# Choice and gate table in one stage with 80 candidate pairs per head, 67 early up products instead of 97, and late ones spread through the experts

## The reference, cut to what matters

```python
q = (xt @ w_q).reshape(t, PEER_HEADS, 2, PEER_HALF)               # 8 heads, 2 halves of 128
sc = jnp.einsum("thpc,hpnc->thpn", q, sub_keys)                   # 128 sub-keys per half
top_s, top_i = lax.top_k(sc, PEER_TOPK)                           # 16 of 128, 16 lists
cand_s = top_s[:, :, 0, :, None] + top_s[:, :, 1, None, :]        # 16 x 16 pairs per head
best_s, best_pos = lax.top_k(cand_s.reshape(t, 8, 256), PEER_TOPK)
idx = ...            # expert = first key * 128 + second key
gate = jax.nn.softmax(best_s, axis=-1)
act = jnp.einsum("cd,ced->ce", xc, u[ic])                         # 128 chosen experts per token
hid = jax.nn.gelu(act, approximate=False) * gc
out = jnp.einsum("ce,ced->cd", hid, v[ic])
```

## Time and profile before

| | us |
|---|---|
| median of 3 runs | 2569.49 |
| lowest, highest | 2559.23, 2578.27 |
| the profiled execution | 2563.19 |
| its span | 2561.4 |
| TensorE busy | 2373.8 (93%) |
| VectorE busy | 1385.9 (54%) |
| ScalarE busy | 733.4 (29%) |
| GpSimd busy | 397.8 (16%) |

### The profile page before, as it was taken

How to read it: one execution, slowest core, us unless ns; L and a number is a source line. 1 busy time by engine, 2 the same in 40 slices (tenths; PEclk the granted TensorE clock), 3 DMA queues, 4 the chain that set the end, 5 groups by cost and what they waited for, 6 DMA issues and landing times. The chain is left out here.

```text
span 2561.4 us, 26540 instructions
## 1 busy us (share of the span) xinstructions
PE 2373.8 (93%) x10097; PEld 1729.5 (68%) x10097; DVE 1385.9 (54%) x2491; ACT 733.4 (29%) x1327; POOL 397.8 (16%) x305
## 2 busy tenths in 40 slices
PE   7989899899999988888989999999995999989889
PEld 4457666686555555656568888889994898875444
DVE  1335423427987966556267777766676624434331
ACT  1134312322111043525233333333333322211110
POOL 1100000000323233232021111123331000013100
PEclk9999999999999999999989999999997999989899
DMA  4231132113877768786899999977772322120110
GB/s 182 94 95 38 54 132 99 70 62 107 272 254 242 247 194 259 228 261 209 269 366 309 316 311 310 310 257 283 274 280 74 132 99 97 68 107 33 50 66 33
DMA packets 183343, 457.32 MB, mean 179 GB/s; under 512 B 15664, under 2 KB 106032, under 8 KB 176432
## 3 DMA queue, kind: packets, MB, share of 16 engines
q1 hardware_dynamic: 146352, 321.38, 37.2%
q0 software_dynamic: 36864, 134.23, 15.3%
HBM read 408.17 MB, written 47.38 MB: 178 GB/s over the span
## 5 line engine op out<-in xcount | busy, mean ns | idle before, releaser
L759 PE MATMUL bank<-XT,ur 128*128 128x384 f32 x1552 | 524.5, 495 | 28.8 <-DMA ur<-in_u 28.5
L759 PEld LDWEIGHTS bank<-XT,ur 128*128 128x128 f32 x1552 | 293.5, 193 | 233.4 <-DMA ur<-in_u 44.7
L1261 PE MATMUL bank<-Vh,Hh 128*128 128x512 f32 x768 | 299.9, 390 | 13.6 <-DVE Hl L1312 13.6
L1262 PE MATMUL bank<-Vl,Hh 128*128 128x512 f32 x768 | 300.0, 391 | 0.0
L1263 PE MATMUL bank<-Vh,Hl 128*128 128x512 f32 x768 | 299.9, 390 | 0.0
L794 POOL DMA_INDIRECT ring_c<-in_v,gidx x128 | 148.0, 1156 | 501.4 <-DVE x_res L806 389.4
L1310 DVE TENSOR_TENSOR Vl<-Vr,Vh 128x1024 fp32r<-128x1024 f32 x128 | 156.8, 1225 | 116.7 <-ACT Vh L1284 112.1
L1284 ACT ACTIVATE Vh<-Vr 128x1024 fp32r<-128x1024 f32 x128 | 135.5, 1059 | 249.9 <-PE bank L1263 221.2
L1261 PEld LDWEIGHTS bank<-Vh,Hh 128*128 128x128 f32 x768 | 144.6, 188 | 44.3 <-DVE Hl L1312 14.9
L768 ACT ACTIVATE ar<-bank 128x384 f32<-128x384 f32 x97 | 47.5, 490 | 428.8 <-PE bank L759 419.5
L1090 DVE TENSOR_TENSOR hot<-tab_sb,ijg 128x1024 f32<-128x1024 f32 x96 | 113.0, 1218 | 105.1 <-PE bank L1116 98.5
(11 more groups left out here) (306 smaller groups left out, 4076.5 us busy)
## 6 DMA issues: line engine op xcount, KB each, us to landing
ur<-in_u SPq DMA_DIRECT2D x128, 512.0 KB
Vr<-in_v SPq DMA_DIRECT2D x128, 512.0 KB, 5.2
W<-in_w_stream SPq DMA_DIRECT2D x27, 2048.0 KB, 7.5
gates<-stage SPq DMA_DIRECT2D x48, 512.0 KB, 6.3
Gr<-gates SPq DMA_DIRECT2D x128, 192.0 KB
early<-ar SPq DMA_DIRECT2D x97, 192.0 KB
A<-early SPq DMA_DIRECT2D x97, 192.0 KB
w_raw<-in_w_mixer SPq DMA_DIRECT2D x14, 1024.0 KB, 4.9
```

Source lines behind the costliest of these rows:

```text
L759: mm = pe.matmul(c.bank[bank + r][:, 0:DN], c.ur[:, r, k * P:(k + 1) * P], c.XT[:, k, 0:DN], start=k == 0, stop=k == KT - 1)
L1261: pe.matmul(ps, Hh[r][:, tok], Vh[r][:, cut], start=n == 0, stop=False)
L1262: pe.matmul(ps, Hh[r][:, tok], Vl[r][:, cut], start=False, stop=False)
```

## The change

1. The scores move into `phase_query`: after query group g+1, TensorE scores group g for all four tiles (8 records); both ScalarE and VectorE copy scores. The keys have a buffer and a DMA of their own.
2. `phase_choose` and `phase_gates` become `phase_table`. The order is: choose tile 3 (gathered), choose 0, choose 1, slices 0, choose 2, slices 1, slices 2. Its buffers lie in the weight ring `c.W`, in `XT` and in `SC`.
3. 80 candidate pairs per head (2x16, 2x8, 4x4, 8x2) instead of 256; the pair is got back from the position with shifts (11 small operations instead of 3).
4. In `choose`, 9 dots lie in the first links and 14 behind the last one-hot sum; slices have none; 12 dots before slices 2; 14 more at the head of the experts, the remaining 33 among them.
5. ScalarE weighs 5 tokens of a slice, VectorE 3.
6. Early products: (9, 13, 13, 13), 4 in each tile's slices, 4 between slices 1 and slices 2, 3 at the end, 67 in all. Stores: 2 per product after slices 0, 4 per product after slices 1, all 16 at once after slices 2.
7. In the experts 61 are late: the first three, then every second or third, never two in a row from the fifth on. ScalarE makes `Uh` of the next but one right behind the gelu. The dots and adds are spread by a weight of 8 per late and 3 per early expert.

```diff
-E_CHOOSE = (10, 16, 16, 16)
-E_LOOP, E_GAP = 4, 9
-E_GATES = sum(E_CHOOSE)
-EARLY = E_GATES + DT * (E_LOOP + E_GAP)
-DOTS_CHOOSE = 63
-DOTS_GAP = 6
+PAIRS = 5 * TOPK
+E_SCORE, E_SLICES, E_DRAIN, E_LAST = (9, 13, 13, 13), 4, 4, 3
+EARLY = sum(E_SCORE) + DT * E_SLICES + E_DRAIN + E_LAST
+LATE = PK - EARLY
+DOTS_LINK, DOTS_TAIL, DOTS_DRAIN, DOTS_FIRST = 9, 14, 12, 14
+DOTS_TABLE = DT * (DOTS_LINK + DOTS_TAIL) + DOTS_DRAIN
...
+                f = g - 1
+                pe.wait_ge(qd if f % 2 else qa, f // 2 + 1)
+                if f >= 4:
+                    pe.wait_ge(sd if f % 2 else sa, f // 2 - 1)
+                for tt in range(TT):
+                    cut = slice(tt * P, (tt + 1) * P)
+                    mm = pe.matmul(c.bank[4 + f % 4][:, tt * PK:(tt + 1) * PK], qT[:, f % 2, cut], keys[:, f], start=True, stop=True)
+                mm.then_inc(sg, 1)
...
+def phase_table(c, ijg, early, SC, gat):
...
+        # sync
+            turns(E0, EH0 + E_SLICES)
+            sp.wait_ge(copied, 2 * NSL)
+            for i in range(E_SCORE[3]):
+                for j in range(2 * i, min(2 * i + 2, CUTS)):
+                    store(0, j)
+                early.turn(sp, E3 + i)
+            turns(EH1, E_SLICES)
+            sp.wait_ge(copied, 4 * NSL)
+            for i in range(E_DRAIN):
+                for j in range(i * CUTS // E_DRAIN, (i + 1) * CUTS // E_DRAIN):
+                    store(1, j)
+                early.turn(sp, ED + i)
+            turns(EH2, E_SLICES)
+            sp.wait_ge(copied, 6 * NSL)
+            for j in range(CUTS):
+                store(2, j)
+            turns(EL, E_LAST)
...
+        # tensor
+            products(E0, E_SCORE[0])
+            products(E1, E_SCORE[1])
+            turn(1)
+            products(E2, E_SCORE[2])
+            turn(2)
+            slices(0, EH0)
+            products(E3, E_SCORE[3])
+            turn(3)
+            slices(1, EH1)
+            products(ED, E_DRAIN)
+            slices(2, EH2)
+            products(EL, E_LAST)
...
+                for a0, na, nb in ((0, 2, 16), (2, 2, 8), (4, 4, 4), (8, 8, 2)):
+                    o = cand[:, :, put:put + na * nb].rearrange("p h (a b) -> p h a b", b=nb)
+                    left = first[:, :, a0:a0 + na].unsqueeze(3).broadcast_to([P, PH, na, nb])
+                    right = second[:, :, 0:nb].unsqueeze(2).broadcast_to([P, PH, na, nb])
+                    last = dve.tensor_tensor(o, left, right, ALU.add)
+                    put += na * nb
...
+                dots(count["room"] + DOTS_TAIL - count["dot"])
+                gates(n)
...
+            choose(0)
+            for n in (1, 2):
+                count["room"] = count["dot"] + DOTS_LINK
+                choose(n)
+            slices(0)
+            count["room"] = count["dot"] + DOTS_LINK
+            choose(3)
+            slices(1)
+            dots(DOTS_DRAIN)
+            slices(2)
...
 def phase_experts(c, early, gat):
...
+    HEAD = 3
+    late = [p < HEAD or (p - HEAD) * (LATE - HEAD) % (PK - HEAD) < LATE - HEAD for p in range(PK)]
...
+        work = [8 * lates[p + 1] + 3 * (p + 1 - lates[p + 1]) for p in range(PK)]
+        due = [OPS * w // work[-1] for w in work]
...
+            # tensor, expert p
+                if p == 0:
+                    up(1)
+                    up(2)
+                elif p + 1 >= HEAD and p + 1 < PK and late[p + 1]:
+                    up(lates[p + 1])
...
+            # scalar, expert p
                     act.activation(A[r][:], c.bank[m % 2][:, 0:DN], ACT.Gelu).then_inc(gelud, 1)
+                    hi_u(m + 2)
...
+            # vector, ahead of expert 0
+            s, done = DOTS_TABLE, 0
+            for i in range(DOTS_FIRST):
+                if i == DOTS_FIRST // 2:
+                    lo_u(2)
+                gat.dot(dve, s)
+                s += 1
```

More of the change, by code:

```diff
@@ L913, in _, with turns, store @@
         @block.sync
         def _(sp):
+            def turns(e, n):
+                for i in range(n):
+                    early.turn(sp, e + i)
+            def store(tt, j):
+                cut = slice(j * PK // CUTS, (j + 1) * PK // CUTS)
+                sp.dma_start(dest[:, cut, tt * P:(tt + 1) * P], stage[:, cut]).then_inc(early.tabled, 16)
             early.load(sp, 0)
             early.load(sp, 1)
-            for e in range(E_GATES):
-                early.turn(sp, e)
+            turns(E0, EH0 + E_SLICES)
@@ L1131, in weigh, with slices @@
                 last.then_inc(weighed_a, 1)
[L1133 to L1134 removed]
+            def slices(tt, e):
                 weigh(tt * NSL)
                 if tt >= 1:
[L1137 removed]
+                    act.wait_ge(early.tabled, 16 * CUTS * tt)
                 for s in range(NSL):
@@ L1169, in _, with scored @@
-        @block.gpsimd
-        def _(pool):
-            for s in range(DOTS_CHOOSE, SLOTS):
-                gat.fetch(pool, s)
-def phase_experts(c, gat):
+                    if s % (NSL // E_SLICES) == NSL // E_SLICES - 1:
+                        early.gelu(act, e + s * E_SLICES // NSL, EB)
+            def scored(n, e):
+                k = E_SCORE[n] - 4
+                gelus(e, k)
+                exped(n)
+                gelus(e + k, 4)
+                if n >= 1:
+                    turned(n)
@@ L1181, in phase_experts @@
+def phase_experts(c, early, gat):
     nc, t = c.nc, c.t
-    LATE = PK - EARLY
     RV = 3
+    HEAD = 3
+    late = [p < HEAD or (p - HEAD) * (LATE - HEAD) % (PK - HEAD) < LATE - HEAD for p in range(PK)]
+    lates = [sum(late[:p]) for p in range(PK + 1)]
+    assert lates[PK] == LATE
+    index = [EARLY + lates[p] if late[p] else p - lates[p] for p in range(PK)]
+    reads = [sum(not late[q] for q in range(p % RV, p + 1, RV)) for p in range(PK)]
     with ExitStack() as ctx:
@@ L1189, in phase_experts @@
         Ul = [sb(f"Ul{i}", [P, KT, P], F32R) for i in range(2)]
+        A = [sb(f"A{i}", [P, DN]) for i in range(RV)]
+        ring = sb("ring", [P, RG, D])
         Vr = [sb(f"Vr{i}", [P, D]) for i in range(RV)]
@@ L1316, in _ @@
-                lo_u(m + 2)
-                due = SLOTS if n == PK - 1 else min(SLOTS, 2 * min(n + 1, EARLY) // 3 + 2 * max(0, n + 1 - EARLY))
-                while done < due:
+                if late[p] and p > 0:
+                    lo_u(lates[p] + 2)
+                while s < SLOTS and s - DOTS_TABLE - DOTS_FIRST < due[p]:
+                    gat.dot(dve, s)
+                    s += 1
+                if p == turn + 2:
+                    dve.wait_ge(gat.gelud, 1)
+                    dve.wait_ge(cleared, 1)
+                    dve.tensor_tensor(gat.hid[:], gat.hid[:], gat.gate[:], ALU.mult).then_inc(gat.gated, 1)
+                    dve.wait_ge(gat.gated, 1)
@@ L1319, in _ @@
+                while p > turn + 2 and done < SLOTS and DOTS + done < due[p]:
                     gat.add(dve, done, acc[:] if done % 2 else c.X[:, GT])
```

595 lines of the change are left out of this document (293 added, 302 removed).

## The result

The changed kernel takes 2598.07 us (2591.44 to 2605.86, six runs), the kernel before beside it 2567.06 (2559.23 to 2578.27): a ratio of 1.0109, with a 95% interval of 1.0087 to 1.0131. I had forecast 2560 us, 3 less than the profiled execution of the kernel before; by the ratio it is 28 us slower. The profiled execution took 2598.08 us, its span 2595.9.

What follows compares the result with a forecast made beforehand. TensorE and VectorE were taken as nearly level, TensorE bounding the experts. First main at 1137.4 + 769.7 of products + 38 of waits = 1945 against 1947.6, so 2563.2 - 3 = 2560 us; range 2515 to 2600.

Steps and rivals of the forecast that it cites:

- gap 0: Between slices 0 and slices 1: 13 products, eight at 6.4 us beside stores, 77 us, level with VectorE's 77.1.
- gap 1 and slices 2: Behind slices 1: 14.3 MB at some 370 GB/s, 38.5 us until stage is free, TensorE waiting some 10; slices end at 1070.2.
- end of the table: After slices 2: last u issued behind all 16 stores, 28 us with the load; TensorE waits some 17, ends at 1103.4.
- start of the experts: Before the first main: u lands, splits, 14 dots on VectorE; 34 us, of which TensorE works 12.6; first main at 1137.4.
- TensorE's ledger: From 585 to the last main: 1234 us of work and 126 standing, against 1261 and 102 before; products alone give -29.4 us.
- the places of the waits: TensorE stands: query's end and choice 25 us, gap 0 11, gap 1 12, table's end 17, experts' start 21, experts 38.
- the cause that I gave: In late experts with an early neighbour, Hl comes 4.31 us after the up against one main of 4.13; 17 us in all.
- ten at 1.7: In the experts, about ten places where two early ones follow a late one: TensorE waits 1.7 us each, 17 in all.
- rival 3: DMA rate decides: gap 0 costs 10 us more, gap 1 50 instead of 38.5, the end 5 more; 2586 us, chance 0.16.
- The tails: 14 dots in a row behind a choice tile's last sum, eight waiting for GpSimd's fetches: 20.5 us, bounds 16.0 and 25.2.
- Rivals 1 and 2: 1: waits hidden in experts, 2510 us, chance 0.27. 2: VectorE late for late experts' gelu, 2630 or 2600 us, 0.15.
- rival 2: In the experts, VectorE's adds make it late for late experts' gelu: +70 us, 2630, or 2600 if half do; chance 0.15.

Runs made afterwards that it cites:

- the late block: Changed kernel with its 58 remaining late experts in one row at the end instead of every second or third: ratio 0.9965 to the kernel before.
- the move of Uh: Changed kernel with ScalarE splitting a late expert's next u behind Hh instead of ahead of Vh, expert 0 excepted: ratio 1.0014 to the kernel before.
- The two kernels on gap 0: Changed kernel without dots and gathers in the choice's third tile: gap 71.2 us; changed kernel with an eighth of the stores behind slices 0: gap 80.8 us.
- short tails: Changed kernel with two dots instead of 14 behind each tile of the choice, the other 36 done in the experts: ratio 1.0072 to the kernel before.
- three edits and short tails: Changed kernel with late experts in one row, last u ahead of 12 stores, two dots before expert 0 and two behind each tile: 2522.37 us, ratio 0.9811.

## Why the prediction was wrong, step by step

| step | predicted | measured | miss |
|---|---|---|---|
| choice begins | 601.5 | 602.4 | +0.9 |
| first tile | 45.4 | 45.6 | +0.2 |
| second, third tile with tails | 78.0, 77.1 | 85.9, 79.0 | +9.8 |
| slices 0 and 1 | 51.2 each | 50.6, 48.2 | -3.6 |
| gap 0 | 78.0 | 88.9 | +10.9 |
| gap 1 and slices 2 | 83.8 | 92.7 | +8.9 |
| end of the table | 33.2 | 40.9 | +7.7 |
| start of the experts | 34.0 | 36.9 | +2.9 |
| experts, to the end of the last main | 807.7 | 804.9 | -2.8 |

These add up to 34.9 us (the slices' begin, four us behind the third tile, was right). Another 2.2 lie behind the last main, where both kernels do the same. Together they are the 37.1 us between the span that the forecast meant (2561.4 less 2.6) and the 2595.9 measured.

**What was right.** TensorE's ledger, the choice's tile, the slices (3.08 us each, 3.2 forecast), the places of the waits but for one of 8.06 us for a `u` in gap 1, and the experts' total, which the late block and the move of Uh trace to the cause that I gave. Its parts were mixed: 20 us on isolated late experts instead of 17, and 13 at nine places that I had counted as ten at 1.7. That the total came out within 3 us is partly luck.

**The step that failed** is the sum's treatment of the DMA engines: "I take 6.4 us for each of the eight: 51 + 26 = 77 us, level with VectorE's", and "some 370 GB/s are 38.5 us, and `stage` is not free before". I put 9 of the third tile's 23 gathers beside the eight products with stores, and left the five products behind them at 5.2 us. In these 26 us lie the 14 gathers of the tail and five loads and gelus, 10.9 MB by my own sizes: 420 GB/s, for which the sum has no term, where 338 were reached over the gap. Measured are 54.8 and 30.5 us, and 3.7, of which I had only 0.8: the rest of the slices' product and the step to the next slices. The stage came free 46.0 us behind slices 1 (1004.6 to the end of TensorE's wait at 1050.56), in which 15.2 MB went at 330 GB/s, not 14.3 at 370. TensorE waited 20.9 us for the last `u`, not 17. These three places are 27.5 of the 34.9 us. The two kernels on gap 0 show the size of it: stores without gathers 71.2 us, both 88.9.

This is rival 3, the DMA rate, to which I gave 0.16: it had 10, 11.5 and 5 us more in these three places; measured are 11, 7.5 and some 4 in the wait with 3 in the product behind it. I weighed it too low because the earlier trace rows showed a full DMA share with TensorE never idle. The share was full in gap 0 too (0.97 over 867 to 957): it tells nothing of how late one given transfer is. What made a given `u` late has no term of its own in the sum: in gap 0 its way from issue to landing, 12.1 us ahead of the longest wait and 6.0 to 7.8 in the tail instead of 4.0; in gap 1 the 13.65 us in which SyncE was held at the issue of the stores ahead of it. Only at the end did I count the stores ahead, 28 us with the load, and it took 32.5 from the last slice to the product's start.

**The tails.** I took 20.5 us for 14 dots, between bounds of 16.0 and 25.2. Measured are 25.7, 23.3 and 23.2. Two dots in the second tile's links waited 3.9 us for rows besides; the sum has nothing for them. The first tail reaches the upper bound, which is also what the rule of the Trainium skill ("SBUF — State Buffer", "SBUF: two separate sides") would give. But its rows show something else than a fetch of 1.99 us each time: most of the late fetches took 0.94 us, and VectorE waited for rows that had been issued but had not landed (in this tail the median from issue to landing was 9.3 us for rows in `W` and 9.8 for rows in `SC`). The runs don't separate the two.

**The clock.** I named a fall of the clock in the new gaps as something that would make me wrong, and put nothing into the sum for it. In the earlier trace rows the granted clock is 0.98 to 0.99; in the changed kernel's stages 0.96, 0.96, 0.71 and 0.79. After the wait of 20.85 us TensorE ran at half speed, 1.2 instead of 2.4 GHz, for 6.1 us, after the 6.24 for 5.4, and so on, eleven times between 603 and 1180 us, 50 us of matmuls in all. In the same stages of the kernel before there were seven, 26 us in all. At half of these lengths, the changed kernel loses 25 us by it and the one before 13: 12 us of the difference, which lie in the misses above beside the waits. They are worked out from these rows; no run isolates them.

**Rivals 1 and 2.** The waits were not hidden; they could have been (the late block). VectorE was not late for the gelu of late experts: it waited for all 58 of them, 195.3 us in all, and moving Uh alone would else have changed nothing.

The range, 2515 to 2600, held the time by 2 us, which is luck: its upper end came from rival 2, which is not what happened. The sign I had wrong. Of the chances, "slower by over 1%" had 0.18.

## What to carry to other kernels

Sum all bytes that fall into a stretch, gathers included, and hold them against the rate that was reached with full engines (330 to 340 GB/s here). Then price a transfer that someone waits for by its place in its queue and by how long the issue of what stands ahead of it takes. Where a run of stores, gathers and a load that TensorE needs meet, ask first whether the gathers can go elsewhere. When an order is spread evenly, look at the shortest distance between an operation and its user that it creates, not at the mean: 35 us of waiting, 20 of them as 0.35 us on each of 56 neighbours, ate the whole gain of 29 us in TensorE's ledger, and one instruction moved on an engine that is busy 264 of 805 us gave most of it back. Behind each wait of several microseconds, add the slow product that follows it.

## What was unexpected of the hardware

Issuing is not free when the DMA engines are full. A store of the last row of 16 took 24.40 / 16 = 1.5 us to issue and one of the four in gap 1 13.65 / 4 = 3.4, against 0.7 in gap 0 without gathers (1.43 for two). A single load took 9.63 us beside gathers, against 0.33 us in the earlier trace rows. SyncE issues in order, so whatever stands behind goes out later by all of it.

In the tail above a gathered row's fetch took 0.94 us on GpSimd where VectorE waited, 1.98 to 1.99 us in the row of busy dots, and lengths between them where the two met in part. The same 128 fetches of the experts have a mean of 1955 ns in the changed kernel, with VectorE busy 532 of 805 us; where short tails and the late block are combined, 1277 ns, with VectorE busier. The late block alone, with VectorE busy 538 us, has 1254 ns. So it is not how busy VectorE is on the whole; that it is the moment at which a fetch falls is my reading, and no run isolates it.

```profile
L793 POOL DMA_INDIRECT ring<-in_v,gidx x128 | 250.2, 1955 | 401.8 <-DVE x_res L805 193.5
```
```profile
L793 POOL DMA_INDIRECT ring<-in_v,gidx x128 | 163.5, 1277 | 280.3 <-DVE x_res L805 133.4
```

(The second row is of the kernel with three edits and short tails.)
